# A hybrid decoder step on one core: page-key rounds of two pairs in place of four, a key ring four rounds deep, and keys turned one round ahead

## What is computed

```
h  = rmsnorm(x);  u = h @ w_in                      # 1024 -> 3584 columns (28 tiles of 128)
a  = differential attention(q, k, v)                # 4 heads, two 64-wide maps per head
     prompt: causal over 1024 tokens
     sample: over 2048 cached tokens (16 pages of 128 per sequence, by page_table) + 4 new ones
b  = mLSTM(conv(xb), gates), chunkwise scan         # 4 heads, matrix memory 128x128
x += rmsnorm([a*silu(za), b*silu(zb)] @ w_out)
x += rmsnorm(sigmoid(x @ ple_gate) * (p @ ple_w))
```

## Time and profile before

| | |
|---|---|
| median of 3 runs | 1055.27 us (1053.37 to 1057.66) |
| the profiled execution | 1053.59 us, of it span 1052.0 us |
| PE, matmuls | 900.0 us busy, 86% |
| PE, weight loads | 711.4 us, 68% |
| DVE | 519.4 us, 49% |
| ACT | 356.4 us, 34% |
| POOL | 161.1 us, 15% |
| mean granted PE clock | 0.946 of 2.4 GHz |
| HBM traffic | 134 GB/s over the span |

### The profile page before, as it was taken

One profiled execution on the slowest core, in us unless ns is written; L12 is line 12 of the kernel. 1 busy time (PEld: TensorE's weight loads), 2 busy tenths in 40 slices (PEclk: granted clock), 3 DMA queues, 4 the chain that ended last, 5 costly groups with the idle time before them and its releaser, 6 DMA issues. The chain is left out here.

```text
span 1052.0 us, 20262 instructions
## 1 busy us (share of the span) xinstructions
PE 900.0 (86%) x8003; PEld 711.4 (68%) x8003; DVE 519.4 (49%) x1066; ACT 356.4 (34%) x777; POOL 161.1 (15%) x338
## 2 busy tenths in 40 slices
PE   4899999999667667999996665877998999999996
PEld 4899889999445445778775343555666787677774
DVE  5644745545165343454555776544667444352222
ACT  5444433334111023353335331433556232322111
POOL 2300000000412110000004233122342000000000
PEclk9999999999878888999998898999998999999998
DMA  7352225222744451222208557576894721113131
GB/s 230 80 157 81 61 73 130 61 61 61 243 130 155 156 195 41 60 61 69 73 21 300 189 154 252 183 234 202 273 393 171 285 80 65 56 55 110 67 109 40
DMA packets 109737, 142.48 MB, mean 135 GB/s; under 512 B 9719, under 2 KB 75895, under 8 KB 109642
## 3 DMA queue, kind: packets, MB, share of 16 engines
q1 hardware_dynamic: 96842, 99.23, 29.6%
q0 software_dynamic: 12800, 41.95, 11.4%
HBM read 125.34 MB, written 15.41 MB: 134 GB/s over the span
## 5 line engine op out<-in xcount | busy, mean ns | idle before, releaser
L2073 PE MATMUL ps<-hhi,whi 128*128 128x272 f32 (+1 forms) x672 | 231.1, 344 | 1.8 <-DVE hlo L1392 1.4
L2073 PE MATMUL ps<-hhi,wlo 128*128 128x272 f32 (+1 forms) x672 | 219.3, 326 | 0.0
L2073 PE MATMUL ps<-hlo,whi 128*128 128x272 f32 (+1 forms) x672 | 219.2, 326 | 0.0
L2073 PE MATMUL ps<-wh,r 128*128 128x512 f32 (+1 forms) x544 | 155.0, 401 | 0.3 <-DVE wout_lo L1953 0.2
L1408 DVE TENSOR_TENSOR wlo<-wst,whi 128x1024 fp32r<-128x1024 f32 x56 | 68.8, 1229 | 156.6 <-ACT whi L995 156.6
L2073 PEld LDWEIGHTS ps<-hhi,whi 128*128 128x128 f32 x672 | 129.0, 192 | 20.7 <-issue 9.3
L2073 PEld LDWEIGHTS ps<-hlo,whi 128*128 128x128 f32 x672 | 129.0, 192 | 10.1 <-issue 2.2
L2073 PEld LDWEIGHTS ps<-hhi,wlo 128*128 128x128 f32 x672 | 128.4, 191 | 9.7
L2073 PEld LDWEIGHTS ps<-wh,r 128*128 128x128 f32 (+1 forms) x544 | 99.1, 185 | 27.0 <-issue 1.6
L785 POOL TENSOR_TENSOR small<-small 128x1 f32<-128x1 f32 (+2 forms) x37 | 7.9, 213 | 480.0 <-ACT junk L1327 198.2
L2073 PE MATMUL ps<-window_keys,qk 32*32 32x256 f32 x1024 | 34.2, 597 | 39.0 <-DVE window_keys L1784 39.0
(11 more groups left out here) (367 smaller groups left out, 1428.4 us busy)
## 6 DMA issues: line engine op xcount, KB each, us to landing
wst<-in_w_in SPq DMA_DIRECT2D x56, 512.0 KB, 3.8
window_keys<-in_cache_k POOLq DMA_DIRECT2D x48, 256.0 KB, 4.6
Kr<-in_cache_k POOLq DMA_DIRECT2D x48, 256.0 KB, 5.9
Vr<-in_cache_v SPq DMA_DIRECT2D x32, 256.0 KB, 3.8
Vr<-in_cache_v POOLq DMA_DIRECT2D x32, 256.0 KB, 4.5
Kr<-in_cache_v SPq DMA_DIRECT2D x32, 256.0 KB, 4.7
Kr<-in_cache_v POOLq DMA_DIRECT2D x32, 256.0 KB, 5.4
out_y_prompt<-rows SPq DMA_DIRECT2D x16, 512.0 KB, 2.9
```

The lines of the kernel that those rows point to most:

```text
L2073: return nc.tensor.matmul(out, lhsT, rhs, start=start, stop=stop, **more)
```

## The change

Rounds become two pairs (4 pages, 1 MB), so there are 32, 16 in each batch. The ring still holds eight pairs and is now four rounds deep: the pages of round g wait for the scores of round g - 4. Each `scores(g)` still has 64 matmuls, with 128 moving columns in place of 256. SP and POOL take one pair each of every round. In the window DVE turns round g + 1 before the convolution and the weight split of round g, PE follows each round by one piece in place of two, and the scores of round g need only round g turned. In the attention a round is scored one decode step later after its last pair is turned (`LAG`), `KEY_SHARE` is 0.36, and the first value pages are issued under finer waits. The page table lies in another order in `ptab` to suit (six small loads, as before).

```diff
-PER_ROUND = 2
+PER_ROUND = 1
-ROUND = GROUPS // 2
+ROUND = GROUPS // 4
+IN_SEQ = GROUPS // ROUND
-RING = 2 * ROUND
+RING = 8
+RING_ROUNDS = RING // ROUND
+LAG = 1
 def round_step(g):
-    return ROUND * (g + 1)
+    return ROUND * (g + 1) + LAG
-VALUE_STEP = [(KEY_STEPS + 4, KEY_STEPS + 6)[m // IN_BATCH] + m for m in range(KEY_STEPS)]
+VALUE_STEP = [(EXP_STEP + 2, EXP_STEP + 4)[m // IN_BATCH] + m for m in range(KEY_STEPS)]
+LAST_KEYS = round_step(ROUNDS - RING_ROUNDS - 1)
+VALUE_WAIT = (0, 0, ROUNDS - 3, ROUNDS - 3, ROUNDS - 2, ROUNDS - 2, ROUNDS, ROUNDS)
-KEY_SHARE = 0.32
+KEY_SHARE = 0.36
...
 # SP
-                    sp.wait_ge(s["scores_ready"], n // ROUND - 1)
+                    sp.wait_ge(s["scores_ready"], n // ROUND - RING_ROUNDS + 1)
-            key_pages(0)
-            key_pages(ROUND)
+            for g in range(RING_ROUNDS):
+                key_pages(ROUND * g)
             for w in range(NT + 3, NT + 6):
                 load_w(w)
-            for g in range(2, IN_ROUNDS):
+            for g in range(RING_ROUNDS, IN_ROUNDS):
                 key_pages(ROUND * g)
-                load_w(NT + 4 + g)
+                if g % 2:
+                    load_w(NT + 4 + g // 2)
...
 # POOL
-            round_pages(0)
+            for g in range(RING_ROUNDS):
+                key_pages(ROUND * g + 1)
             nc.gpsimd.memset(qk[0][:], 0.0).then_inc(s["zero_ready"], 1)
-            round_pages(1)
             pool.wait_ge(*done["q_rep_stored"])
             own_queries(0)
...
 # DVE, the window
-            for g in range(IN_ROUNDS):
+            def round_turned(g):
                 for n in range(ROUND * g, ROUND * g + ROUND):
                     keys_turned(n)
-                if g + 1 < H:
-                    conv_second(g + 1)
+            round_turned(0)
+            for g in range(IN_ROUNDS):
+                if g + 1 < IN_ROUNDS:
+                    round_turned(g + 1)
+                if g % 2 and g // 2 + 1 < H:
+                    conv_second(g // 2 + 1)
                 fill(PER_ROUND)
...
 # PE
-                j, half = divmod(r, 2)
+                j, part = divmod(r, IN_SEQ)
+                width = 32 * GP * ROUND
...
-                            last = mm(ps[32 * h:32 * h + 32, score_bank(b, a), 256 * half:256 * half + 256]...
+                            last = mm(ps[32 * h:32 * h + 32, score_bank(b, a), width * part:width * part + width]...
...
-                if n % ROUND == 0 and IN_BATCH < n <= KEY_STEPS:
-                    scores(n // ROUND - 1)
+                if n in SCORES_AT:
+                    scores(SCORES_AT[n])
```

More of the change, by code:

```diff
@@ L121 @@
 TURNS_AT = {n: [bt for bt in TURNS if TURN_STEP[bt] == n] for n in range(STEPS_OF_DECODE)}
-VALUE_ISSUE = [KEY_STEPS - 2 * ROUND + 1 + q if q < 2 else round_step(ROUNDS - 2) + q - 1 if q < 6 else
-               round_step(ROUNDS - 1) + q - 5 if q < RING else VALUE_STEP[q - RING] + 1 for q in range(KEY_STEPS)]
+SCORES_AT = {round_step(g): g for g in range(IN_ROUNDS, ROUNDS)}
+LAST_KEYS = round_step(ROUNDS - RING_ROUNDS - 1)
+VALUE_WAIT = (0, 0, ROUNDS - 3, ROUNDS - 3, ROUNDS - 2, ROUNDS - 2, ROUNDS, ROUNDS)
+VALUE_ISSUE = [max(LAST_KEYS, round_step(VALUE_WAIT[q] - 1)) + 1 + q % 2 if q < RING else VALUE_STEP[q - RING] + 1
+               for q in range(KEY_STEPS)]
 VALUES_ISSUED_AT = {n: [q for q in range(KEY_STEPS) if VALUE_ISSUE[q] == n] for n in range(STEPS_OF_DECODE)}
@@ L571, in _ @@
                 load_w(w)
[L572 to L576, removed]
             load_heads(1)
@@ L582, in _ @@
             for turn in range(2):
+                first = KEY_STEPS * turn
+                sp.dma_start(ptab[0:1, first:first + KEY_STEPS].rearrange("o (b g k) -> o b g k", b=NSEQ, k=GP),
+                             io["page_table"][:, :].rearrange("(o b) (g q k) -> o q b g k", o=1, q=2, k=GP)[:, turn, :, :, :]
+                             ).then_inc(s["ptab_in"], 16)
                 for b in range(BATCHES):
@@ L614, in _ @@
             sp.wait_ge(s["wqkv_in"], 64 + 64)
-            key_pages(0)
-            key_pages(ROUND)
+            for g in range(RING_ROUNDS):
+                key_pages(ROUND * g)
             for w in range(NT + 3, NT + 6):
                 load_w(w)
-            for g in range(2, IN_ROUNDS):
+            for g in range(RING_ROUNDS, IN_ROUNDS):
                 key_pages(ROUND * g)
-                load_w(NT + 4 + g)
-            for w in range(NT + 4 + IN_ROUNDS, WEIGHTS):
+                if g % 2:
+                    load_w(NT + 4 + g // 2)
+            for w in range(NT + 4 + IN_ROUNDS // 2, WEIGHTS):
                 load_w(w)
@@ L628, in value_pages @@
                 if q < RING:
-                    sp.wait_ge(s["scores_ready"], ROUNDS if q >= 6 else ROUNDS - 1)
+                    if VALUE_WAIT[q]:
+                        sp.wait_ge(s["scores_ready"], VALUE_WAIT[q])
                 else:
@@ L637, in _ @@
             sp.wait_ge(s["piece_done"], EVENTS)
-            for g in range(IN_ROUNDS, IN_ROUNDS + 2):
+            for g in range(IN_ROUNDS, IN_ROUNDS + RING_ROUNDS):
                 key_pages(ROUND * g)
@@ L646, in _ @@
                 for n in range(DECODED[pos - 1] if pos else IN_BATCH, DECODED[pos]):
-                    if n % ROUND == 0 and IN_BATCH < n <= KEY_STEPS - RING:
-                        key_pages(n + ROUND)
+                    if n in SCORES_AT and SCORES_AT[n] + RING_ROUNDS < ROUNDS:
+                        key_pages(ROUND * (SCORES_AT[n] + RING_ROUNDS))
                     for q in VALUES_ISSUED_AT[n]:
@@ L864, in key_pages @@
             def key_pages(n):
-                turn = 3 * (n // ROUND) + n % ROUND - 1
+                turn = n // ROUND
                 if turn % 4 == 0:
-                    own_pages(32 + GP * turn)
+                    own_pages(KEY_STEPS + GP * turn)
                 if n >= RING:
-                    pool.wait_ge(s["scores_ready"], n // ROUND - 1)
+                    pool.wait_ge(s["scores_ready"], n // ROUND - RING_ROUNDS + 1)
                 for k in range(GP):
@@ L873, in key_pages @@
                                         ).then_inc(k_in[n % RING], 16)
-            def round_pages(g):
-                for n in range(ROUND * g + 1, ROUND * g + ROUND):
-                    key_pages(n)
             def own_queries(b):
@@ L903, in _ @@
                                             ).then_inc(s["q8_ready"], 1)
-            for g in range(2, IN_ROUNDS):
-                round_pages(g)
+            for g in range(RING_ROUNDS, IN_ROUNDS):
+                key_pages(ROUND * g + 1)
             for i in range(H, CH):
@@ L916, in value_pages @@
                 if q < RING:
-                    pool.wait_ge(s["scores_ready"], ROUNDS if q >= 6 else ROUNDS - 1)
+                    if VALUE_WAIT[q]:
+                        pool.wait_ge(s["scores_ready"], VALUE_WAIT[q])
                 else:
@@ L953, in _ @@
                 for n in range(DECODED[pos - 1] if pos else IN_BATCH, DECODED[pos]):
-                    if n % ROUND == 0 and IN_BATCH < n <= KEY_STEPS - RING:
-                        round_pages(n // ROUND + 1)
+                    if n in SCORES_AT and SCORES_AT[n] + RING_ROUNDS < ROUNDS:
+                        key_pages(ROUND * (SCORES_AT[n] + RING_ROUNDS) + 1)
                     for q in VALUES_ISSUED_AT[n]:
@@ L1180, in _ @@
                 fill(PER_ROUND)
-                if g == 5:
+                if g == 11:
                     act.wait_ge(s["conv_step"], CONV_SECOND)
                     copy(xch_[1][:, :, :], xch_[1][:, :, :], "silu_ready", ACT.Silu)
-                if g == 6:
+                if g == 13:
                     gate_tiles(OB, 1, ACT.Sigmoid)
@@ L2331, in scores @@
                     pe.wait_ge(s["q8_ready"], NSEQ + 2 * PACK * (1, 3)[b])
-                pages = slice(GROUPS * half, GROUPS * half + GROUPS)
+                first_page = GP * ROUND * (g % RING_ROUNDS)
+                pages = slice(first_page, first_page + GP * ROUND)
                 for c in range(H):
@@ L2337, in scores @@
                             first = h * DH + 32 * c
-                            last = mm(ps[32 * h:32 * h + 32, score_bank(b, a), 256 * half:256 * half + 256].rearrange("p (g t) -> p g t", t=32),
+                            last = mm(ps[32 * h:32 * h + 32, score_bank(b, a), width * part:width * part + width].rearrange("p (g t) -> p g t", t=32),
                                       qk[b][rows, j, h, c, :], key_ring(IN_BATCH * b)[rows, pages, first:first + 32],
```

## The result

| | before | after |
|---|---|---|
| median | 1054.61 us (1053.37 to 1057.66, 4 runs) | 1024.54 us (1022.44 to 1028.52, 4 runs) |
| ratio | | 0.9715, 95% interval 0.9676 to 0.9755 |
| the profiled execution | 1053.59 us, span 1052.0 | 1028.52 us, span 1026.9 |

Faster by 30.1 us, against 39.4 forecast; 1016 had been named, with 1003 to 1045 as the range. The page of the profile after, the line that answers to the earlier trace rows: busy us, share, instructions.

A forecast was written before the change was run, and what follows sets the result against it. PE's work plus its waits bound the kernel, window key waits coming from DVE's order. Window 71.6 and attention 40.2, less 2 and 32 s (s = 2.2), save 39.4 us: 1016 us, 8-in-10 range 1003 to 1045.

The forecast's parts named there:

- the rival of issue: Key rounds: instruction issue sets the round, so s stays 2.69 us; 23.7 us saved, 1032 us; chance 0.17.
- the prediction's own sum: Whole kernel: 109.8 - 32 s saved, 39.4 us with s = 2.2, giving 1016 us.
- The bound: Window: PE's 39.0 us of waits for turned keys come from DVE's stream order, not bandwidth.
- s: Time from a half-column key round's start to what follows: taken as 2.2 us, lower bound 1.83, upper 3.83.
- tile model: Key rounds: eight matmuls per array tile, each paying weight load and columns; half the columns gives 1.83 us at full clock.
- the burst of the earlier trace: PE: 16 instructions in about 0.4 us, some 13 ns each; 128 would take 2.1 us with drain.
- The window: First round to next chunk: 71.6 - 16 s saved, 36.4 us with s = 2.2, allowing 2 us of stalls.
- The start: Window's first round: 2.4 us earlier; weight tile behind eight page DMAs counted at nothing, 1.5 us either way.
- The attention: Attention key rounds: 40.2 - 16 s saved, 5.0 us, with 11 us of key waits and 3 of row-minima waits removed.
- Squeezing the values: Attention's values stretch: squeezing it by 4% costs 0 to 5 us, taken as 2.
- Keys set the pace: Rival, window and attention: waits for turned keys become waits for landed ones; 13 us saved, about 1042 us; chance 0.14.
- Narrow rounds dear: Rival, key rounds: narrow rounds lower the clock and cost 3.83 us each; 1068 us, slower; chance 0.09.

The follow-up runs named there:

- e6: Kernel before with one edit: DVE turns window round g + 1 ahead of round g's convolution and weight rest; 1013.07 us, ratio 0.9602.
- e5: e2 with DVE's window order of before, each round turned in its own turn; 1048.41 us, ratio 0.9928.
- e1: Changed kernel, but in the window DVE turns round g in its own turn, not round g + 1; 1024.95 us, ratio 0.9699.
- e4: Changed kernel with each round's scores multiplied in two halves of 64 columns, 512 instructions in place of 256; 1154.87 us, ratio 1.0935.
- e9: e2 with each four-pair round multiplied in two halves of 128 columns; 1057.2 us, ratio 1.0036.
- e2: Changed kernel with rounds of four pairs (256 columns), still turned ahead, SP and POOL issuing two pairs each; 1002.93 us, ratio 0.949.
- e3: Changed kernel loading only 64 of 512 columns of each key page behind the first ring; 1009.93 us, ratio 0.958.
- e7: Changed kernel with the attention plan of before, KEY_SHARE 0.32 and LAG 0; 1027.61 us, ratio 0.9727.
- e8: e2 with SP loading the weight tile ahead of the first key ring in place of behind it; 1001.11 us, ratio 0.9477.
- e10: e8 with KEY_SHARE 0.32 in place of 0.36; 1001.6 us, ratio 0.9519.

## Why the prediction was right, and where its sum was off

**Two errors of opposite sign.** The time fell into the range, but that it did is in part luck. By the time alone the rival of issue (1032 us) is as near as the forecast (1016), and it is the length of a clean round that tells them apart. The rounds were cheaper than forecast, 1.83 us in place of 2.2, which by the prediction's own sum is 32 x 0.37 = 11.8 us more saved and a time of 1004. The measured one lies 20 us above that. The 16.8 us of waits for instructions, which the sum did not have, are most of the difference.

**The bound was read rightly.** The window's waits were an order in DVE's stream: e6 changes that order alone and the 39.0 us become 4.7, e5 puts it back and they are 37.5. (All of e6's 4.7 us stand ahead of the first round.) What the prediction did not see is that the change cures one wait twice. Small rounds (e1) or turning ahead (e6) do it alone, and the small rounds are the costly one of the two. (A small round and a ring four rounds deep come together in e1; they were not told apart.)

**The round of half the columns.** s was taken as 2.2, with 1.83 as the tile model's value. Clean rounds measure 1.83 in window and attention, 554.18 to 556.01 in the second:

```profile
554.18 1.90 PE L2083 MATMUL ps<-Kr,qk 32*32 32x128 f32 x128
556.01 1.13 PE L2083 MATMUL ps<-U 64*128 64x512 f32 x4
```

The tile model (eight matmuls one after another on each tile, each a weight load and its columns) gave this value before it was measured, and the burst of the earlier trace rows, some 13 ns, was no evidence of a limit. e4 agrees with the model at 64 columns. The rival of issue at a fixed cost per instruction falls.

**What took its place: the supply of instructions.** This term was not in the sum. The page counts a queue "instruction" (packets, MB, share of the DMA engines), here of after:

```profile
q8 instruction: 79, 1.29, 0.5%
```

Before it has 63 packets. The change adds 4096 instructions on PE and 16 packets of 16 KB, so a packet holds 256; e4 adds 12288 to the kernel before and has 111 packets, 48 more. 0.5% of 16 engines' span for 79 packets is about 1 us for each. Nine issue waits in the key rounds of after are over 0.4 us; eight end 1.2 to 1.6 us after such a packet has landed, and so do 16 of 17 in e9. The wait at 338.97 has its packet in this stretch of 336 to 338 us, while PE stood still:

```profile
q8 instruction: 1, 0.02, 3.1%
```

A narrow round uses up 256 instructions in 1.83 us, a wide one in 2.69, and the same number of columns needs twice as many. The waits grow with that demand (16.8, 31.0 and 81.3 us in `after`, e9 and e4, next to none in e2) and nearly vanish in the window when the key traffic is taken away (e3). That packets come late because they share the DMA engines with the keys is only half of it, as three windows show, the first two of `after`, the third of e9:

```profile
331.00:336.50 5.50, 3.97 (x128) 2.96 (x128) 3.98 (x4) 0.00 (x0) 0.72 (x2) 1.00 0.90 280
337.00:339.00 2.00, 0.03 (x5) 0.03 (x4) 0.00 (x0) 0.00 (x0) 0.00 (x0) 1.00 0.03 4
658.50:662.90 4.40, 2.52 (x173) 1.89 (x153) 1.44 (x2) 1.67 (x4) 0.00 (x0) 1.00 0.02 4
```

The packet that ends the wait at 338.97 is not slow. It takes 1 us, but it starts at the end of a burst of keys that filled the DMA engines, when they are nearly free again. Yet in e9 PE waits 1.85 us, up to 662.94, while the DMA engines carry nothing but the packet itself. So a long wait behind a burst fits the sharing, and a wait of 1 to 2 us also comes without it, where only the demand of narrow matmuls is left to explain it. Why the packet starts no sooner there, and whether behind a burst it is the queues of the DMA engines or the HBM that holds it, stays open. The Trainium skill, "Runtime: NRT & Kernel Launch", section "Instruction fetch mechanics", says that an engine fetches its stream in blocks of 256 instructions by itself and that the cost is mostly hidden, because the engine dispatches more slowly than it is refilled. The traces agree on the 256 and not on the hiding: at 10 to 14 ns per pair of matmul and weight load PE stood still for 16.8 to 81.3 us.

**The window, 5.5 us short.** Sixteen rounds of 4.78 are 76.5 of the 88.5 us, less than the 80 of the forecast: 1.83 and not 2.2 for the round, but 2.95 and not 2.8 for the piece (309.43 to 312.38). The other 12.0 are 6.6 of issue waits, 1.5 of a first round at low clock (6.26 to the second one), 0.6 at the end, 1.9 of low clock behind the 3.32 us wait, and 1.4 in short halts that the list of waits does not show. 2 us for all stalls had been allowed.

**The start, 2.0 us short.** The weight tile that stands behind eight page DMAs in SP's queue was counted at nothing, with 1.5 us either way. ACT starts its split at 292.15 in place of 290.34, 1.8 us later. But this is one run of each: e1, e3, e4 and e7, which are the same as `after` up to here, start their first round at 299.64, 298.89, 300.05 and 301.65 where `after` has 301.34, and e6, the same as before, at 301.13 where that has 301.79. A shift of 2 us is no more than this scatter; the means of five and of two runs are 300.3 and 301.5, 1.1 us apart. That the tile's place matters is shown by e8 and e10 against e2, e5 and e9 alone.

**The attention, 8.1 us short.** The rounds' busy time was sized well, 36.1 us against 35.2. The waits for `Kr` went entirely, 14.4 and not 11. PE's short waits for row minima did not shrink, 20.5 us against 20.2 before, where 3 us had been hoped for: that a round would fill them was argued from a plan and not from a row. And 10.3 us of issue waits came, with the clock down to 0.77 in 600 to 625 us. From the first `Kr` round to the output (before, then after) the clock is 0.94 and 0.91:

```profile
574.82:801.00 226.18, 174.46 (x2755) 114.76 (x2754) 139.40 (x356) 90.87 (x250) 65.17 (x121) 0.94 0.70 238
545.79:777.00 231.21, 190.65 (x3779) 130.10 (x3778) 139.95 (x356) 91.05 (x250) 58.17 (x109) 0.91 0.70 232
```

PE is busy 16.2 us more (9.9 in rounds, 6.3 in the other matmuls, which are as many as before and run at the lower clock) and idle 11.1 less: +5.1. A part of the lesser idling had not been counted: PE's waits for the tile `on` from DVE fall from 7.4 to 1.0 us. Squeezing the values cost little: their stretch moves 345 GB/s at a DMA share of 0.95, and PE waits 2.3 us for them, against 1.4.

**The rivals.** Issue as a fixed cost per instruction: refuted by e4. Keys set the pace: no wait of PE or DVE of any size names them; 209 GB/s was enough, in the window, where 260 had been forecast. Narrow rounds dear: the size was wrong for `after`, since clean rounds cost 1.83 and not 3.83, but its direction holds. e9, with wide rounds cut in halves, loses 54 us to e2, more than all that e2 had gained. The clock does not fall because the rounds are narrow, as that rival had it: in e3 the narrow rounds run through the window at 1.00 behind the first, with PE busy 72.4 of 73 us. In `after` it is 0.5 for a while behind the 3.32 us wait, and 1.00 from there to the window's end, with the wait of 1.57 us in it (e3, then after):

```profile
306.00:379.00 73.00, 72.42 (x2101) 55.61 (x2100) 48.06 (x57) 20.03 (x21) 12.00 (x22) 1.00 0.31 82
344.00:389.00 45.00, 43.43 (x1260) 33.23 (x1252) 23.69 (x24) 15.59 (x15) 5.38 (x10) 1.00 0.57 179
```

**What beats both.** Wide rounds turned ahead with even issue: 1002.93 us (e2) and 1001.11 with the weight tile first (e8). Even the single edit of e6, at 1013.07, beats the whole change.

## What to carry to other kernels

When a change cures a wait by two means, price each alone: here reordering one engine's stream cost nothing and brought 42 us, and cutting the rounds in half brought nothing on top but cost PE 0.97 us for every two small rounds, and waits for instructions. Count the instructions per microsecond that small tiles ask for, not only their busy time, above all where DMA is heavy: a wait named "issue" in the middle of a run of equal matmuls, with packets of the instruction queue landing just ahead of its end, is the mark of it. A transfer that the critical path waits for belongs ahead of bulk loads in its queue, even when the bytes are the same in sum: here it brought the window forward by at least 4.6 us, though the whole time not by more than its noise. And compare starts over several runs of the same program before a shift of 2 us is given a cause.

## What the runs showed of the hardware

- The rows fit a model in which matmuls on one 32x32 tile of the array run one after another, each with its weight load, 107 ns plus two cycles per column, and sixteen tiles run side by side. For 128 matmuls that is 2.76 us at 256 columns and 1.91 at 128, with 0.2 of drain, where the rows have 2.76 and 1.90; at 64 columns it is 10 ns per matmul, where e4 has 9.8. The Trainium skill, "TensorE: Matmul & The Clock Gate", section "Wait - 56ns, not 53.3ns?", has starts never less than about 25 ns apart; by the row at 309.04 of e4 they are 9.8 ns apart.
- PE can run out of instructions: up to 5.3 us at a time, 81.3 us in all (e4), with packets of 256 instructions landing 1.2 to 1.6 us ahead of the end of nearly every wait. It does so with the DMA engines otherwise idle too, 1.85 us up to 662.94 in e9.
- A long stall can cost more than its length. After the 3.3 us at 338.97 the clock was at 1.2 GHz for some eight matmuls of the projection, 0.43 us from start to start in place of 0.23, another 1.5 us. Behind the 1.57 us at 365.57 it stayed at 2.4 GHz.
